# A float32 two-block transformer kernel: sixteen modulation chunks load into a buffer of their own

## The chip, the cores and the metric

The kernel runs on one core of a Trainium2 chip. The metric is device time in microseconds from the first to the last instruction of the core, with what the launch adds around it. The engines are TensorE (PE; its weight loads are PEld), VectorE (DVE), ScalarE (ACT), GpSimd (POOL) and SyncE (SP), whose queue issues nearly all of the weight transfers.

## The reference

Two blocks run over 256 positions of width 2048, all in float32: an attention block with an FFN, then an mLSTM block with a gated convolution. Both are modulated by a condition vector `c`. Of the first block, cut to what matters here:

```python
mod = silu(c) @ w_ada + b_ada
sh_a, sc_a, gt_a, sh_f, sc_f, gt_f = split(mod, 6)
h = rmsnorm(x, g_pre_attn) * (1 + sc_a) + sh_a
proj = h @ w_in                       # 2048 x 6144
mix = concat([dilated_attention(...), differential_attention(...)])
x = x + gt_a * rmsnorm(mix @ w_out, g_post_attn)
h = rmsnorm(x, g_pre_ffn) * (1 + sc_f) + sh_f
x = x + gt_f * rmsnorm((silu(h @ w_gate) * (h @ w_up)) @ w_down, g_post_ffn)
```

The product with `w_ada` is matrix times vector: its 96 chunks for this block (48 more belong to the second block) of 128 x 2048 floats are read once each.

## The kernel before

**Weights.** Every weight matrix comes as chunks of 1 MiB (128 partitions x 2048 floats) into one of four slots of the tile RAW. A chunk is two halves of 1024 columns. Each half is split in two parts so that float32 accuracy is kept: ACT copies it rounded into HI (`hi_half`, L668), DVE subtracts and writes the rest into LO (`split_half`, L1625), and TensorE does three products per half (`narrow`; HI with the high and the low part of the activations at L1200 and L1201, LO with the high part at L1209). HI and LO have four half-slots each, so ACT and DVE run at most four halves ahead of TensorE.

**Modulation.** A modulation chunk needs no TensorE: DVE multiplies it with the condition vector and sums over the row in one instruction, in place (`ada_chunk`, L1635), and adds 1 to the semaphore `ada_step`.

**Order.** `first_body()` writes out the order of the first section, "W" for a weight chunk and "A" for a modulation chunk. From chunk 16 on each W is followed by the A's that `ADA_BEHIND` gives it: one for chunks 18 to 61, two for 48, 50, 52 and 54. The class `Section` gives item j of that list the slot j mod 4; the load of an item waits until the item four places before it is used up (`slot_free`): by DVE's split for a W (`lo_ready`), by DVE's product for an A (`ada_step`). With W and A in turn, the four slots hold two of each. SP walks through the list in order: wait for the slot, issue the load, next item (`slot_wait`, `load` at L561). DVE walks through the same list: two splits for a W, and behind each half what else is due at that half (`beside_first(h)`); for an A its product.

**What else is due.** The first section has 64 weight chunks, halves 0 to 127. Halves 0 to 95 are the input projection, 96 to 127 the output projection. Beside them run the attention steps, placed by the half's number. Those that matter here: `rope` on DVE writes rotated queries and keys into QKY (two tiles of 1024 floats), TensorE turns them, ACT's `qk_evac` (L799) reads the turned ones out and adds 1 to `qt_ready` (16 in all, the last at half 88). `dilated_pv` (L1380) waits through `bank_7_free` until ACT has taken the head before (`dilated_out`, L850). `head_rstd` on DVE (L2000) precedes `head_norm` on ACT (L871), which precedes `mixa_turn` on TensorE (L1402), which precedes `mixa_hi` (L887) and on DVE `mixa_low` (L1899, halves 103 and 111). `out_gain` on DVE (L2015, halves 116 and 120) takes a group's outcome out of the two banks that TensorE's halves 116 and 120 start to fill again; TensorE waits for it (`wo_out`). At the end TensorE does the first 128 rows of halves 124 to 127 ahead of the second 128 rows.

**Memory.** The tile R is cut into regions by hand. QKY lies at 12288 to 14335. C_ROW_2, the condition of the second block, lies at 13312 and is loaded once the first section is over.

Of the kernel before, what the change touches and what calls it, by code (L numbers as in the profile page):

```python
# [52 lines left out]
RAWS = 4  # L53
HLS = 4
# [34 lines left out]
DIRECT_PAIRS = 6  # L89

ADA_BEHIND = sorted(list(range(18, 62)) + [48, 50, 52, 54])

UNITS_AT = 40

# [143 lines left out]
class Section:  # L238


    def __init__(self, plan, name, body, n_iter, groups=0):
        self.name, self.body, self.n_iter, self.groups = name, body, n_iter, groups
        self.n_chunks = len(body)
        self.n_halves = 2 * sum(kind == "W" for kind, *_ in body)
        self.n_ada = sum(kind == "A" for kind, *_ in body)
        assert self.n_chunks % RAWS == 0 and self.n_halves % HLS == 0
        self.chunk0, self.half0, self.ada0, self.group0 = plan.chunks, plan.halves, plan.ada, plan.groups
        self.items, half, ada = [], 0, 0
        slot_gain = [0] * RAWS
        for j, (kind, *what) in enumerate(body):  # L250
            slot = j % RAWS
            slot_gain[slot] += 16
            self.items.append(dict(kind=kind, what=what, slot=slot, j=j, half=half, ada=ada,
                                   landed=slot_gain[slot]))
            if kind == "W":
                half += 2
            else:
                ada += 1
        self.slot_gain = slot_gain
        self.landed0 = list(plan.landed)  # L260
        self.before = list(plan.last)
        n = n_iter
        plan.chunks += n * self.n_chunks
        plan.halves += n * self.n_halves
        plan.ada += n * self.n_ada
        plan.groups += n * groups
        for s in range(RAWS):
            plan.landed[s] += n * slot_gain[s]
        plan.last = [self.freed(self.items[j], n - 1) for j in range(self.n_chunks - RAWS, self.n_chunks)]

    def freed(self, it, i):

# [11 lines left out]
        return self.group0 + i * self.groups + off  # L284

    def landed(self, i, it):
        return self.landed0[it["slot"]] + i * self.slot_gain[it["slot"]] + it["landed"]

    def slot_free(self, i, it):
        j = it["j"] - RAWS  # L290
        if j >= 0:
            return self.freed(self.items[j], i)
        if isinstance(i, int) and i == 0:
            return self.before[it["j"]]
        return self.freed(self.items[self.n_chunks + j], i - 1)


class Plan:
    def __init__(self):
        self.chunks = self.halves = self.ada = self.groups = 0  # L300
        self.landed = [0] * RAWS
        self.last = [None] * RAWS


def first_body():

    body = [("A",)] * 4
    for n in range(8):
        ahead = [("A",)] * (2 if n < 7 else 0)
        if n == 0:  # L310
            body += [("W", 0)] + ahead + [("W", 1)] + ahead
            continue
        if n == 6:
            body += ahead + [("W", 2 * n), ("W", 2 * n + 1)] + ahead
            continue
        body += ahead + [("W", 2 * n)] + ahead + [("W", 2 * n + 1)]
    for c in range(16, 64):
        body.append(("W", c))
        body += [("A",)] * ADA_BEHIND.count(c)
    return body  # L320


# [39 lines left out]
def build(nc, x, c_rows, pos_cols, smalls, lambda_q1, lambda_k1, lambda_q2, lambda_k2,  # L362
# [4 lines left out]
    with ctx:  # L367
# [5 lines left out]
        def sem(name):  # L373
            return ctx.enter_context(nc.semaphore(name))

        PS = ctx.enter_context(nc.psum_tensor("PS", [P, 8, 512], F32))
        RAW = sb("RAW", [P, RAWS, 2048])
# [41 lines left out]
        def region(at, *shape):  # L419
            n = int(np.prod(shape))  # L420
            assert at + n <= RF, (at, shape)
            v = R[:, at:at + n]
            if len(shape) == 2:
                return v.rearrange("p (a b) -> p a b", a=shape[0])
            if len(shape) == 3:
                return v.rearrange("p (a b c) -> p a b c", a=shape[0], b=shape[1])
            return v
# [17 lines left out]
        MTB = region(8192, NH, S)  # L445
        GGA = region(10240, 2048)
        QKY = [region(12288 + 1024 * n, NT, 512) for n in range(2)]
        ROT = region(14336, 2, 512)
        JUNKW = region(14336, 2, 512)
        PX = region(15360, 4, 256)  # L450
# [51 lines left out]
            sum_m en_ready if_cols mq_ready ms_done w_x w_e pm_ready mpv_done mo_done  # L502
            zb_silu conv_in conv_t conv_y conv_ready o_sig h_gated mssq m_ms m_root m_rstd z_silu
            ha_ready hat_ready gates_sig merged merge_t mt_ready rows_2 sq_2 x_normf normf_in out_ready last_ready out_done""".split()
        landed = [sem(f"landed{i}") for i in range(RAWS)]
        bias_in = [sem(f"bias_in{i}") for i in range(4)]

        s = namedtuple("Semaphores", names)(*[sem(n) for n in names])
# [28 lines left out]
        def as_it_is(h):  # L537

            n, g = divmod(h, EARLY)
            return WHOLE[:, (n * len(DIRECT) + DIRECT.index(g)) % 4, :]  # L540

        def bank_of(g):
            return 2 * (g % 2)

# [13 lines left out]
        @block.sync  # L558
        def _(sp):
            def load(sec, it, chunk):  # L560
                sp.dma_start(RAW[:, it["slot"], :], chunk).then_inc(landed[it["slot"]], 16)  # L561

            def ada_dma(sec, it):
                load(sec, it, w_mod[sec.ada_chunk(0, it["ada"])])

            def slot_wait(sec, it):
                freed = sec.slot_free(0, it)
                if freed is not None:
                    sp.wait_ge({"W": s.lo_ready, "D": s.hi_ready, "A": s.ada_step}[freed[0]], freed[1])

            sp.dma_start(C_IN, c_rows[0:1, :]).then_inc(s.c_in, 16)
            sec = secs["first"]
            for it in sec.items:
                slot_wait(sec, it)
                if it["kind"] == "A":
                    ada_dma(sec, it)
                    if it["j"] == 0:
                        for u in range(NT):
                            sp.dma_start(X[:, u, :], x[0, u * P:(u + 1) * P, :]).then_inc((s.x_in, s.x_in_1)[u], 16)
                    continue  # L580
                load(sec, it, w_first[it["what"][0]])
            sec = secs["ffn"]
            for it in sec.items:
                slot_wait(sec, it)
                if it["kind"] == "A":
                    ada_dma(sec, it)
                    continue
                load(sec, it, w_ffn[it["half"] // 2])
            sec = secs["down"]
            for it in sec.items:  # L590
                slot_wait(sec, it)
                if it["kind"] == "A":
                    ada_dma(sec, it)
                    continue
                load(sec, it, w_down[it["what"][0]])
            sp.wait_ge(s.ada_step, ADA_OF_C)
            sec = secs["second"]
            for it in sec.items:
                g, k = it["what"]
                _, at = source_of(g)  # L600
                if k == 0 and g < PROJ_B:
                    if g >= 4:
                        sp.wait_ge(s.group_out, left(g - 4))
                    sp.dma_start(BIAS4[:, g % 4, :], b_in_2[0:1, at:at + 512].to_broadcast([P, 512]))\
                      .then_inc(bias_in[g % 4], 16)
                freed = sec.slot_free(0, it)
                sp.wait_ge(s.lo_ready if freed[0] == "W" else s.ada_step, freed[1])
                load(sec, it, w_second[it["half"] // 2])
            for n, (u, cols) in enumerate(((0, slice(0, 1024)), (0, slice(1024, 2048)), (1, slice(0, 512)), (1, slice(512, 1280)))):
                sp.wait_ge(s.out_ready, n + 1)  # L610
                sp.dma_start(out[0, u * P:(u + 1) * P, cols], X[:, u, cols]).then_inc(s.out_done, 16)
            sp.wait_ge(s.out_done, 80)
# [1000 lines left out]
        def _(dve):  # L1613
# [14 lines left out]
            def ada_chunk(sec, it):  # L1628

                a = sec.ada_chunk(0, it["ada"])  # L1630
                w = RAW[:, it["slot"], :]
                dve.wait_ge(landed[it["slot"]], sec.landed(0, it))
                if a == ADA_OF_C:
                    dve.wait_ge(s.cact_ready, 2)
                dve.tensor_tensor_reduce(w, w, C_ROW if a < ADA_OF_C else C_ROW_2, 1.0, 0.0, ALU.mult, ALU.add,  # L1635
                                         MOD[:, a:a + 1]).then_inc(s.ada_step, 1)
                for n, at in enumerate(GATE_AT):
                    if a == at + NK - 1:
                        gate(n)
                if a == MOD_AT[1] + 31:  # L1640
                    modulation(2)
# [188 lines left out]
            sec = secs["first"]  # L1830
# [270 lines left out]
            sec = secs["ffn"]  # L2101
# [18 lines left out]
            sec = secs["second"]  # L2120
# [253 lines left out]
            for h in range(HALVES_2 + EVAC):  # L2374
                g, n = divmod(h, 8)
# [135 lines left out]
```

## Time and profile before

| | us |
|---|---|
| median of 3 runs | 2382.34 (2380.48 to 2387.35) |
| the profiled execution | 2381.54 |
| its span, first to last instruction | 2379.7 |
| PE busy in the span | 2334.0 (98%) |
| DVE busy in the span | 1815.3 (76%) |
| ACT busy in the span | 1121.4 (47%) |
| transfers | 598.47 MB, 251 GB/s over the span |

A row of a page or a view has the line of the kernel behind an L, the engine, the operation and its tiles. An idle time in brackets is how long the engine stood still before the row, with what released it. A busy PE isn't PE at its peak: ends of matmuls are modelled.

### The profile page before, as it was taken

To read this page: it belongs to the slowest core of one execution; us is meant where nothing else is said; L and a number is where in the kernel's file an instruction comes from. 1 tells how busy PE (TensorE), PEld (TensorE's weight loads), DVE (VectorE), ACT (ScalarE), POOL (GpSimd) and SP (SyncE) were. 2 spreads that over 40 slices of the span, in tenths; PEclk is the share of its full clock that TensorE was granted. 3 is DMA by queue.
4 is the path that set the end of the run, shared out by engine and by line. 5 is a ranking of instruction groups with operands and counts; after the bars stand their busy time and mean duration, and the time that the engine had idled before them with its cause. 6 is when DMAs were issued, how large, how long until landed. Compare 5 with 4: busy or idle time off the path is not lost.

```text
span 2379.7 us, 26167 instructions
## 1 busy us (share of the span) xinstructions
PE 2334.0 (98%) x10274; PEld 1887.7 (79%) x10274; DVE 1815.3 (76%) x2441; ACT 1121.4 (47%) x1471; POOL 14.7 (1%) x31
## 2 busy tenths in 40 slices
PE   7999999999999999999999999999999999999998
PEld 3377787878888888888878888888888888888887
DVE  6698988878888888987665577998767795555775
ACT  5445566464444444444464434444345544444453
POOL 0000000000000000000000000000000000000000
PEclk8999999999999999999999999999999999999999
DMA  9988889877787777888746555555666657555553
GB/s 375 421 295 309 293 321 341 327 266 284 281 300 283 283 281 284 305 331 316 267 155 203 199 199 193 190 191 203 208 208 208 202 193 258 200 192 192 189 194 123
DMA packets 87757, 598.47 MB, mean 251 GB/s; under 512 B 10145, under 2 KB 10209, under 8 KB 16593
## 3 DMA queue, kind: packets, MB, share of 16 engines
q1 hardware_dynamic: 85538, 588.95, 68.8%
q0 software_dynamic: 1664, 7.19, 0.9%
q8 instruction: 81, 1.33, 0.2%
q10 hardware_dynamic: 432, 0.66, 0.1%
q14 instruction: 42, 0.34, 0.0%
HBM read 594.62 MB, written 2.13 MB: 251 GB/s over the span
## 4 chain that ended last, share of the span: by engine, by line
PE 89%; DVE 5%; DMA 4%; ACT 1%; issue 1%; DVEq 0%; ACTq 0%
PE PS L1184 20%; PE PS L1200 19%; PE PS L1201 19%; PE PS L1209 19%; PE PS L1189 10%; DVE RAW L1635 2%; DMA RAW<-in_w_first 2%; DMA RAW<-in_w_mod 2%; DVE LO L1625 1%; PE PS L1329 1%; PE PS L1548 0%; DVE X L1714 0%; ACT R L665 0%; ACT HI L668 0%; PE PS L1279 0%
## 5 line engine op out<-in xcount | busy, mean ns | idle before, releaser
L668 ACT ACTIVATE HI<-RAW 128x1024 fp32r<-128x1024 f32 x784 | 828.2, 1059 | 1096.0 <-PE PS L1209 669.2
L1625 DVE TENSOR_TENSOR LO<-RAW,HI 128x1024 fp32r<-128x1024 f32 x784 | 956.5, 1223 | 464.1 <-ACT HI L668 460.4
L1200 PE MATMUL PS<-HI,XH 128*128 128x512 f32 x2080 | 822.5, 395 | 4.9 <-DVE XL L1888 1.6
L1201 PE MATMUL PS<-HI,XL 128*128 128x512 f32 x2080 | 811.2, 390 | 0.0
L1209 PE MATMUL PS<-LO,XH 128*128 128x512 f32 x2080 | 559.1, 390 | 1.1 <-DVE LO L1625 1.1
L1200 PEld LDWEIGHTS PS<-HI,XH 128*128 128x128 f32 x2080 | 390.8, 188 | 90.1 <-DVE XL L1888 4.0
L1209 PEld LDWEIGHTS PS<-LO,XH 128*128 128x128 f32 x2080 | 391.0, 188 | 83.5 <-DVE LO L1625 1.6
L1201 PEld LDWEIGHTS PS<-HI,XL 128*128 128x128 f32 x2080 | 391.1, 188 | 79.0
L1184 PE MATMUL PS<-HI,XH 128*128 128x512 f32 x1056 | 325.9, 390 | 1.6 <-DVE XL L1735 1.1
L1184 PE MATMUL PS<-HI,XL 128*128 128x512 f32 x1056 | 325.2, 389 | 0.0
L1189 PE MATMUL PS<-LO,XH 128*128 128x512 f32 x1056 | 283.9, 389 | 0.0
L1635 DVE CUSTOM_DVE_ANT_0 RAW<-RAW,BIAS 128x2048 f32<-128x2048 f32 x96 | 218.9, 2287 | 32.7 <-DMA RAW<-in_w_mod 24.3
L1665 DVE STREAM_TRANSPOSE R<-R 32x256 f32<-32x256 f32 (+1 forms) x608 | 230.8, 380 | 12.7
L1184 PEld LDWEIGHTS PS<-HI,XH 128*128 128x128 f32 x1056 | 197.7, 188 | 42.6 <-DVE XL L1735 1.3
L1184 PEld LDWEIGHTS PS<-HI,XL 128*128 128x128 f32 x1056 | 198.3, 188 | 41.2
L1189 PEld LDWEIGHTS PS<-LO,XH 128*128 128x128 f32 x1056 | 198.2, 188 | 41.3 <-DVE LO L1625 0.2
L1635 DVE CUSTOM_DVE_ANT_0 RAW<-RAW,R 128x2048 f32<-128x2048 f32 x48 | 109.9, 2289 | 0.5
L1224 PE MATMUL PS<-R 128*128 128x512 f32 x192 | 87.1, 609 | 7.9 <-ACT XH L787 5.0
L1224 PEld LDWEIGHTS PS<-R 128*128 128x128 f32 x192 | 36.5, 194 | 58.0 <-issue 52.2
L665 ACT ACTIVATE R<-RAW 128x1024 f32<-128x1024 f32 x24 | 24.1, 1048 | 45.9 <-DMA RAW<-in_w_first 45.8
L2307 DVE TENSOR_TENSOR R<-PS,BIAS 128x1024 f32<-128x1024 f32 x24 | 29.2, 1216 | 0.0
L737 ACT ACTIVATE R<-PS,MOD,SCALE 128x256 f32<-128x256 f32 (+1 forms) x38 | 18.0, 525 | 14.4 <-PE PS L1279 14.4
(258 smaller groups left out, 876.2 us busy)
## 6 DMA issues: line engine op xcount, KB each, us to landing
RAW<-in_w_second SPq DMA_DIRECT2D x208, 1024.0 KB, 4.8
RAW<-in_w_mod SPq DMA_DIRECT2D x144, 1024.0 KB, 5.5
RAW<-in_w_ffn SPq DMA_DIRECT2D x88, 1024.0 KB, 4.9
RAW<-in_w_first SPq DMA_DIRECT2D x64, 1024.0 KB, 6.2
RAW<-in_w_down SPq DMA_DIRECT2D x44, 1024.0 KB, 5.1
BIAS<-in_b_in SPq DMA_DIRECT2D x40, 256.0 KB, 5.1
R<-mod_rows POOLq DMA_DIRECT2D x3, 1024.0 KB, 7.4
X<-in_x SPq DMA_DIRECT2D x2, 1024.0 KB, 8.8
```

The lines of the kernel that those rows point to most:

```text
L665: act.activation(as_it_is(h), whole, ACT.Copy).then_inc(s.hi_ready, 1)
L668: act.activation(HI[:, (it["half"] + hf) % HLS, :], whole, ACT.Copy).then_inc(s.hi_ready, 1)
L1184: pe.matmul(PS[:, bank_of(u, cc), :], x, HI[:, slot, cc * 512:(cc + 1) * 512], start=first and x is xh, stop=False)
L1189: m = pe.matmul(PS[:, bank_of(u, cc), :], XH[:, slot_k, u * P:(u + 1) * P], LO[:, slot, cc * 512:(cc + 1) * 512], start=False, stop=last)
L1200: pe.matmul(PS[:, bank + u, :], XH[:, 2 * n + kk, rows], hi, start=start and kk == 0, stop=False)
L1201: pe.matmul(PS[:, bank + u, :], XL[:, 2 * n + kk, rows], hi, start=False, stop=False)
L1209: m = pe.matmul(PS[:, bank + u, :], XH[:, 2 * n + kk, u * P:(u + 1) * P], lo, start=False, stop=stop and kk == 1)
L1224: m = pe.matmul(PS[:, bank + u, :], XT[:, 2 * n + kk, u * P:(u + 1) * P], as_it_is(h)[:, kk * 512:(kk + 1) * 512], start=start and kk == 0 ...
L1625: dve.tensor_tensor(LO[:, slot, :], RAW[:, it["slot"], hf * 1024:(hf + 1) * 1024], HI[:, slot, :].bitcast(F32), ALU.subtract).then_inc(s.l ...
L1635: dve.tensor_tensor_reduce(w, w, C_ROW if a < ADA_OF_C else C_ROW_2, 1.0, 0.0, ALU.mult, ALU.add, MOD[:, a:a + 1]).then_inc(s.ada_step, 1)
L1665: m = dve.transpose(columns(b, a), rows(a, b))
L2307: dve.tensor_tensor(dst, y, bias, ALU.add).then_inc(s.group_out, 1)
```

## The change

Sixteen modulation chunks, the first one behind each of the weight chunks 44 to 59, are loaded into a buffer of their own, OWN, at 12288 in R (where QKY lies). The class `Plan` keeps a turn over the four slots for all other items of all sections; the fifth slot, with a semaphore of its own, is OWN. Each item carries the count at which it has landed and what must be used up before its load. SP skips an OWN item in the list and issues its load behind the load of weight chunk c+2; before the first it waits for `qt_ready` 16, before each of the others for the product of the OWN chunk before it. The order of DVE, ACT and TensorE is unchanged. The number of other items in the first section is 128, so later sections keep their slots.

```diff
--- before.py
+++ after.py
@@ -90,6 +90,8 @@
 
 ADA_BEHIND = sorted(list(range(18, 62)) + [48, 50, 52, 54])
 
+OWN_SLOT = range(44, 60)
+
 UNITS_AT = 40
 
 
@@ -243,30 +245,28 @@
         self.n_chunks = len(body)
         self.n_halves = 2 * sum(kind == "W" for kind, *_ in body)
         self.n_ada = sum(kind == "A" for kind, *_ in body)
-        assert self.n_chunks % RAWS == 0 and self.n_halves % HLS == 0
+        assert self.n_halves % HLS == 0
         self.chunk0, self.half0, self.ada0, self.group0 = plan.chunks, plan.halves, plan.ada, plan.groups
         self.items, half, ada = [], 0, 0
-        slot_gain = [0] * RAWS
         for j, (kind, *what) in enumerate(body):
-            slot = j % RAWS
-            slot_gain[slot] += 16
-            self.items.append(dict(kind=kind, what=what, slot=slot, j=j, half=half, ada=ada,
-                                   landed=slot_gain[slot]))
+            if kind == "A" and what:
+                slot = RAWS
+            else:
+                slot = plan.turn % RAWS
+                plan.turn += 1
+            plan.landed[slot] += 16
+            it = dict(kind=kind, what=what, slot=slot, j=j, half=half, ada=ada, landed=plan.landed[slot], free=plan.last[slot])
+            self.items.append(it)
+            plan.last[slot] = self.freed(it, 0)
             if kind == "W":
                 half += 2
             else:
                 ada += 1
-        self.slot_gain = slot_gain
-        self.landed0 = list(plan.landed)
-        self.before = list(plan.last)
         n = n_iter
         plan.chunks += n * self.n_chunks
         plan.halves += n * self.n_halves
         plan.ada += n * self.n_ada
         plan.groups += n * groups
-        for s in range(RAWS):
-            plan.landed[s] += n * slot_gain[s]
-        plan.last = [self.freed(self.items[j], n - 1) for j in range(self.n_chunks - RAWS, self.n_chunks)]
 
     def freed(self, it, i):
 
@@ -284,22 +284,18 @@
         return self.group0 + i * self.groups + off
 
     def landed(self, i, it):
-        return self.landed0[it["slot"]] + i * self.slot_gain[it["slot"]] + it["landed"]
+        return it["landed"]
 
     def slot_free(self, i, it):
-        j = it["j"] - RAWS
-        if j >= 0:
-            return self.freed(self.items[j], i)
-        if isinstance(i, int) and i == 0:
-            return self.before[it["j"]]
-        return self.freed(self.items[self.n_chunks + j], i - 1)
+        return it["free"]
 
 
 class Plan:
     def __init__(self):
         self.chunks = self.halves = self.ada = self.groups = 0
-        self.landed = [0] * RAWS
-        self.last = [None] * RAWS
+        self.landed = [0] * (RAWS + 1)
+        self.last = [None] * (RAWS + 1)
+        self.turn = 0
 
 
 def first_body():
@@ -316,7 +312,9 @@
         body += ahead + [("W", 2 * n)] + ahead + [("W", 2 * n + 1)]
     for c in range(16, 64):
         body.append(("W", c))
-        body += [("A",)] * ADA_BEHIND.count(c)
+        if c in OWN_SLOT:
+            body.append(("A", c))
+        body += [("A",)] * (ADA_BEHIND.count(c) - (c in OWN_SLOT))
     return body
 
 
@@ -445,6 +443,7 @@
         MTB = region(8192, NH, S)
         GGA = region(10240, 2048)
         QKY = [region(12288 + 1024 * n, NT, 512) for n in range(2)]
+        OWN = region(12288, 2048)
         ROT = region(14336, 2, 512)
         JUNKW = region(14336, 2, 512)
         PX = region(15360, 4, 256)
@@ -502,7 +501,7 @@
             sum_m en_ready if_cols mq_ready ms_done w_x w_e pm_ready mpv_done mo_done
             zb_silu conv_in conv_t conv_y conv_ready o_sig h_gated mssq m_ms m_root m_rstd z_silu
             ha_ready hat_ready gates_sig merged merge_t mt_ready rows_2 sq_2 x_normf normf_in out_ready last_ready out_done""".split()
-        landed = [sem(f"landed{i}") for i in range(RAWS)]
+        landed = [sem(f"landed{i}") for i in range(RAWS + 1)]
         bias_in = [sem(f"bias_in{i}") for i in range(4)]
 
         s = namedtuple("Semaphores", names)(*[sem(n) for n in names])
@@ -539,6 +538,9 @@
             n, g = divmod(h, EARLY)
             return WHOLE[:, (n * len(DIRECT) + DIRECT.index(g)) % 4, :]
 
+        def raw_of(it):
+            return OWN if it["slot"] == RAWS else RAW[:, it["slot"], :]
+
         def bank_of(g):
             return 2 * (g % 2)
 
@@ -558,7 +560,7 @@
         @block.sync
         def _(sp):
             def load(sec, it, chunk):
-                sp.dma_start(RAW[:, it["slot"], :], chunk).then_inc(landed[it["slot"]], 16)
+                sp.dma_start(raw_of(it), chunk).then_inc(landed[it["slot"]], 16)
 
             def ada_dma(sec, it):
                 load(sec, it, w_mod[sec.ada_chunk(0, it["ada"])])
@@ -570,7 +572,10 @@
 
             sp.dma_start(C_IN, c_rows[0:1, :]).then_inc(s.c_in, 16)
             sec = secs["first"]
+            own = {it["what"][0]: it for it in sec.items if it["slot"] == RAWS}
             for it in sec.items:
+                if it["slot"] == RAWS:
+                    continue
                 slot_wait(sec, it)
                 if it["kind"] == "A":
                     ada_dma(sec, it)
@@ -579,6 +584,12 @@
                             sp.dma_start(X[:, u, :], x[0, u * P:(u + 1) * P, :]).then_inc((s.x_in, s.x_in_1)[u], 16)
                     continue
                 load(sec, it, w_first[it["what"][0]])
+                c = it["what"][0] - 2
+                if c in own:
+                    if c == OWN_SLOT[0]:
+                        sp.wait_ge(s.qt_ready, 16)
+                    slot_wait(sec, own[c])
+                    ada_dma(sec, own[c])
             sec = secs["ffn"]
             for it in sec.items:
                 slot_wait(sec, it)
@@ -1628,7 +1639,7 @@
             def ada_chunk(sec, it):
 
                 a = sec.ada_chunk(0, it["ada"])
-                w = RAW[:, it["slot"], :]
+                w = raw_of(it)
                 dve.wait_ge(landed[it["slot"]], sec.landed(0, it))
                 if a == ADA_OF_C:
                     dve.wait_ge(s.cact_ready, 2)
```

## Rows read from the trace of the kernel before

**Rows 1.** The page, part 1: busy time of each engine.
```profile
PE 2334.0 (98%) x10274; PEld 1887.7 (79%) x10274; DVE 1815.3 (76%) x2441; ACT 1121.4 (47%) x1471; POOL 14.7 (1%) x31
```

**Rows 2.** Busy time by stretch: stretch, length, engines, granted clock, DMA share, GB/s.
```profile
345.50:390.50 45.00, 42.82 (x231) 36.35 (x229) 37.87 (x58) 33.35 (x77) 0.00 (x0) 1.00 0.87 324
390.50:449.70 59.20, 56.69 (x258) 46.48 (x256) 52.06 (x54) 29.33 (x58) 0.00 (x0) 1.00 0.97 368
449.70:466.20 16.50, 16.50 (x74) 13.69 (x73) 14.64 (x15) 7.26 (x10) 0.00 (x0) 1.00 0.97 359
```

**Rows 3.** Waits of PE from 330 to 470 us: total, times, longest.
```profile
PE PS L1380 <- ACT R L850: 2.2, 1, 2.2
PE PS L1402 <- ACT R L871: 1.4, 1, 1.4
PE PS L1200 <- DVE XL L1899: 1.1, 1, 1.1
```

**Rows 4.** Timeline, all engines, 380 to 410 us: start, length, instruction, idle before it.
```profile
380.02 2.29 DVE L1635 CUSTOM_DVE_ANT_0 RAW<-RAW,BIAS 128x2048 f32<-128x2048 f32 x1
...
382.35 0.33 SPq L561 DMA_DIRECT2D RAW<-in_w_first  x1
...
384.93 0.33 SPq L561 DMA_DIRECT2D RAW<-in_w_mod  x1
...
387.24 1.06 ACT L668 ACTIVATE HI<-RAW 128x1024 fp32r<-128x1024 f32 x1 [0.98 <-DMA RAW<-in_w_first]
...
409.45 1.06 ACT L668 ACTIVATE HI<-RAW 128x1024 fp32r<-128x1024 f32 x1 [4.18 <-DMA RAW<-in_w_first]
```

**Rows 5.** Loads: modulation from 500 to 900, from 400 to 430; RAW from 370 to 420.
```profile
RAW<-in_w_mod SPq DMA_DIRECT2D x34, 1024.0 KB, 4.9
...
RAW<-in_w_mod SPq DMA_DIRECT2D x6, 1024.0 KB, 7.7
...
DMA to landing us min/median/max: 4.8/6.5/8.6
```

**Rows 6.** Timeline of DVE: first modulation products behind chunks 44, 48, 50, 52, 54, 55, 59.
```profile
342.05 2.29 DVE L1635 CUSTOM_DVE_ANT_0 RAW<-RAW,BIAS 128x2048 f32<-128x2048 f32 x1
...
371.65 2.28 DVE L1635 CUSTOM_DVE_ANT_0 RAW<-RAW,BIAS 128x2048 f32<-128x2048 f32 x1
...
384.83 2.28 DVE L1635 CUSTOM_DVE_ANT_0 RAW<-RAW,BIAS 128x2048 f32<-128x2048 f32 x1
...
399.41 2.28 DVE L1635 CUSTOM_DVE_ANT_0 RAW<-RAW,BIAS 128x2048 f32<-128x2048 f32 x1
...
413.14 2.28 DVE L1635 CUSTOM_DVE_ANT_0 RAW<-RAW,BIAS 128x2048 f32<-128x2048 f32 x1
...
422.21 2.28 DVE L1635 CUSTOM_DVE_ANT_0 RAW<-RAW,BIAS 128x2048 f32<-128x2048 f32 x1
...
443.21 2.29 DVE L1635 CUSTOM_DVE_ANT_0 RAW<-RAW,BIAS 128x2048 f32<-128x2048 f32 x1
```

**Rows 7.** Timeline of SP and ACT from 337 to 340 us.
```profile
337.12 0.33 SPq L561 DMA_DIRECT2D RAW<-in_w_first  x1
...
338.23 0.58 ACT L799 ACTIVATE R<-PS 128x512 f32<-128x512 f32 x1
...
339.33 0.33 SPq L561 DMA_DIRECT2D RAW<-in_w_mod  x1
```

**Rows 8.** Timeline of DVE and PE from 446 to 450 us.
```profile
446.97 1.23 DVE L1625 TENSOR_TENSOR LO<-RAW,HI 128x1024 fp32r<-128x1024 f32 x1 [1.47 <-ACT HI L668]
448.12 1.22 DVE L2015 TENSOR_TENSOR R<-PS,R 128x1024 f32<-128x1024 f32 x1
...
449.68 0.39 PE L1200 MATMUL PS<-HI,XH 128*128 128x512 f32 x1
```

**Rows 9.** A gap of PE earlier in the section, and the busy time behind it.
```profile
168.40 0.63 PE L1318 MATMUL PS<-SMALLS,R 128*128 128x128 f32 x4 [3.07 <-ACT R L799]
...
170.00:175.00 5.00, 5.00 (x19) 3.98 (x18) 5.00 (x5) 2.13 (x4) 0.00 (x0) 0.71 0.99 395
```

## Prediction

> **What bounds the kernel now.** I read first how busy TensorE is, then where it stands idle near the change, then who made it wait. Over the execution PE is 98% busy [rows 1]. The change touches the first section's last 40 of 128 halves (a chunk of weights is two halves), so I cut the trace there, at TensorE's starts of halves 88, 100 and 120. From 345.5 to 390.5 us twelve halves take 45.0 us, from 390.5 to 449.7 twenty take 59.2 us, all of it at a granted clock of 1.00 [rows 2]. Per chunk that is 7.5 us in the first stretch (attention lies between the products) and 5.92 us in the second. TensorE idles 2.18 us and 2.51 us in them, and not at all in the eight halves behind. The waits name the same places: 2.2, 1.4 and 1.1 us, 4.7 us together [rows 3]. So TensorE sets the pace, with DVE three or four halves ahead of it, and all that could be won in this region is 4.7 us, 0.2%. What can be lost is larger, because DVE is nearly as full (37.9 of 45.0 and 52.1 of 59.2 us [rows 2]) and runs strictly in order: splits of the weights, modulation chunks, attention.
>
> **What the change removes and adds.** The 16 modulation products themselves (L1635, 2.29 us each with the read of the sum) stay on DVE in the same places of its order. Bytes stay the same. Removed: sixteen of the turns in the four slots, so a weight chunk can be loaded up to four weight chunks ahead instead of two. Added: one single buffer for the sixteen, and on SP, in order, a wait for the previous modulation product before each of their loads. SP issues each such load behind weight chunk c+2, but in effect the wait sets its time: the buffer is free only when the product of c-1 is done.
>
> That makes a closed cycle of steps that can't overlap: product, SP's issue, the load, product. The load is the unknown. Its nearest rows: the product that started at 380.02 us released SP, which issued at 382.35 (2.33 us later), and ACT started on that chunk at 387.24 [rows 4]. That is 4.89 us from the issue to its reader's start, although the queue got another load 2.58 us behind it, which is how the new loads will lie. The median of the modulation loads in the FFN section, with one or two loads in flight, is 4.9 us as well; in the crowded stretch from 400 to 430 us it is 7.7 us, because three or four loads queue up there [rows 5]. I take the 4.89, and keep 4.5 and 7.7 for the range. One cycle is then 2.33 + 4.89 = **7.22 us**. Beside TensorE's 7.5 us per chunk it costs nothing; beside 5.92 us it costs 1.3 us per chunk until DVE's lead is gone, and then all of it is TensorE's.
>
> The Trainium skill, "Trainium Kernel Development and Optimization", Best Practices, says to double-buffer so that transfers and compute overlap; a buffer of one, refilled behind its own reader, is the opposite, and the rows above say what that costs here. The Trainium skill, "DMA: Bandwidth & Descriptors", Anatomy of one DMA, fits 2.0 us plus the bytes at 436 GB/s; for 1 MiB that is an estimate of 4.4 us, by which the sum below would be about 8 us. The trace's 4.89 us is used.
>
> **The walk through the sixteen.** Starts of before are the L1635 rows [rows 4, 6]. DVE's work between them keeps its durations: a split takes 1.14 us from start to start, a product 2.2.
> Chunk 44: SP issues W46 at 337.12 and can issue again 2.2 us later, at 339.33, as in before; the last rotated keys have left the buffer at 338.8 (L799, 338.23 + 0.58) [rows 7]. DVE starts at 344.2 against 342.05, +2.2. Four cycles lead to 373.1 for chunk 48, against 371.65, +1.4: the pace there is 7.5 us and the lead hides it. Chunk 48 has a second product in an ordinary slot, and from 48 to 49 DVE has 8.4 us of work of its own, more than a cycle: chunk 49 at 381.5, again +1.5.
> Chunk 50: released at 383.8, started at 388.7, where DVE was ready at 386.3; **+3.9**. On TensorE's side the wait at L1380 may grow: the attention norms on ACT start behind DVE's L2000, some 1.5 us late now, less the 0.98 us that ACT waited for a weight chunk [rows 4] and that the longer look-ahead removes. Chunk 51 by DVE's own work (two products, two splits, two clamps, L1899): 398.0, again +3.8. Chunk 52 by the cycle: 405.2 against 399.41, **+5.8**. Chunk 53, by either, 412.6, +5.7. Chunk 54 by the cycle: 419.8 against 413.14, **+6.7**. Chunk 55 by DVE's own work (two products, two splits, L1899): 427.8 against 422.21, +5.6. TensorE's half 110 waits for that L1899 and is now as late as it.
> Chunks 56 to 59 by the cycle, four times 7.22: 456.7 against 443.21, **+13.5**.
> Then comes the gate that turns this into time. TensorE's half 120, started at 449.68, needs the outcome of DVE's L2015, which ended at 449.3 (448.12 + 1.22) [rows 8]: 0.4 us of slack. Between chunk 59's product and it, DVE idled 1.47 us for ACT [rows 8], and that is eaten first. So half 120 starts 13.5 - 1.47 - 0.4 = **11.6 us** later, at 461.3. The eight halves behind it are back to back in before [rows 2] and stay so, since DVE's own backlog behind the gate, two products and seven splits among it, keeps its length. Everything further is bound by the same chains as before and shifts as a whole; the FFN section has no idle in which to win it back.
>
> What costs nothing, and why: the weight loads come earlier than needed (each is issued at the latest one cycle after its slot, two chunks ahead of use); the wait for the last rotation falls at 338.8, in SP's ordinary pause; the rotation buffer has no other reader after that. ACT's waits for weight chunks vanish, but ACT isn't late except at the L1380 place already counted. The cycle decides at some eight places (50, 52, 53, 54, 56 to 59), so each tenth of a microsecond in the landing moves the sum by 0.8 us.
>
> **The sum** against the profiled execution: 2381.5 + 11.6 = 2393.1. That execution was 0.8 us under the median of the three runs, so by the median 2393.9.
>
> **Rivals.**
> *The longer look-ahead wins (not slower).* If each modulation load landed before DVE reached it, the 2.2 us and parts of the 1.4 and 1.1 us would go: up to 4.7 us less, 2378. For it: ahead of both longer waits ACT had waited for a weight chunk, 0.98 us at 387.24 and 4.18 us at 409.45 [rows 4]. Its point: the cycle would have to be no longer than 5.92 us, so a landing within 3.6 us; no load of weights or modulation from 370 to 420 us landed in under 4.8 us [rows 5]. Chance 0.05.
> *Mostly hidden (slower by less than 7 us).* Landings near 4.2 us, or more of DVE's lead left than I count: 11.6 less 0.8 us per tenth, so 2384 to 2389. Against it stands the same 4.8 us. Chance 0.11.
> *More than forecast.* The new loads meet the weight loads and take 6.5 us, the median from 370 to 420 us [rows 5]: 1.6 us times eight, 2407. Or TensorE's clock falls in the new gaps: after a gap of 3.07 us before 168.40 us the granted clock was 0.71 in the next five [rows 9], while around the gap of 2.2 us in the region it stayed at 1.00 [rows 2, 3]. My gaps are 1 to 3 us; at 0.71 five microseconds lose 1.5, mostly inside time in which TensorE waits anyway. Chance 0.15.
> *The change doesn't do what it says.* The slots don't hold weights alone: four modulation chunks (the second ones of 48, 50, 52, 54) and the last two stay in them, and W45 and W47 still wait for one. It changes no number above.
>
> **How the numbers follow.** Forecast 0.69, with its own range 2391 to 2399 (landing 4.5 to 5.5 us). About 0.3% (7 us) is what a measurement of this kernel tells from no change. Faster by more than that would need more than all the idle there is: 0.02. Within it: most of the first two rivals, 0.14. Slower: 0.84. The range 2387 to 2406 leaves out the first rival, most of the second and the far end of the third.
>
> **What would show it.** In the changed kernel the waits "DVE RAW L1635 from the modulation load" (0.3 us in the region before) should become some 20 us over ten times or more, up to 2.6 us each; the L1635 starts of chunks 56 to 59 should be 7.2 us apart; TensorE should idle 12 to 14 us from half 100 to half 120, not 2.5; ACT's waits for weights of the first section should be near nothing there; half 120 should start at 461 us. I am wrong if the L1635 starts keep a spacing of 5 to 6 us in the last chunks, or if half 120 is late and the end is not.

## The result and the profile after

The changed kernel takes 2411.0 us (median of 4 runs, 2409.8 to 2413.3) against 2383.2 for the kernel before in the same rounds: ratio 1.0121, 95% interval 1.0109 to 1.0133. The ratio makes 28.8 us (these two medians differ by 27.8), where I had forecast 11.6 and a range that ended at 2406. The profiled execution took 2410.6 us with a span of 2408.8, 29.1 more than the span before. Of all executions below one was disturbed, the profiled one of the kernel that keeps TensorE busy: it took 7650 us, the other three 2409 to 2411, and it is left out.

In the changed kernel the lines behind L540 have moved: the product on DVE is L1646 (was L1635), the split L1636 (L1625), the low part of the mixed heads L1910 (L1899), the gain L2026 (L2015), the attention norms L882 (L871), the transposes on TensorE L1391 and L1413 (L1380 and L1402).

The page, part 1, answers to [rows 1]: all engines do the same work in a longer span.

```profile
PE 2341.8 (97%) x10274; PEld 1892.7 (79%) x10274; DVE 1815.6 (75%) x2441; ACT 1122.1 (47%) x1471; POOL 14.7 (1%) x31
```

TensorE's waits of the changed kernel from 330 to 500 us (total, times, longest), which answer to [rows 3]:

```profile
PE PS L1413 <- ACT R L882: 8.7, 1, 8.7
PE PS L1391 <- ACT R L861: 7.0, 2, 6.1
PE PS L1211 <- DVE R L2026: 6.6, 2, 4.5
PE PS L1371 <- DVE SMALL L1946: 1.0, 1, 1.0
PE PS L1211 <- DVE XL L1910: 0.7, 1, 0.7
PE PS L1220 <- DVE LO L1636: 0.5, 1, 0.5
```

They sum to 24.5 us where there were 4.7. Behind nearly all of them stands one wait of DVE, in the same stretch (0.3 us and one time before):

```profile
DVE R L1646 <- DMA R<-in_w_mod: 39.3, 15, 4.9
```

So 15 of the 16 products find their chunk not landed. The longest of TensorE's waits, for instance, comes from there (DVE, ACT and TensorE):

```profile
425.42 2.29 DVE L1646 CUSTOM_DVE_ANT_0 R<-R,BIAS 128x2048 f32<-128x2048 f32 x1 [4.91 <-DMA R<-in_w_mod]
...
429.20 2.44 ACT L882 ACTIVATE R<-R,SMALL 128x128 f32<-128x128 f32 x8 [7.57 <-DVE SMALL L2011]
...
431.70 1.97 PE L1413 MATMUL PS<-SMALLS,R 128*128 128x128 f32 x8 [8.69 <-ACT R L882]
```

DVE waited 4.91 us for the load of this product, `head_rstd` (L2011) follows it on DVE, the norm on ACT waits for that and TensorE for the norm. The next view shows why some of these waits are longer than others. It is the timeline from 368 to 400 us, of SP's issues and DVE's products (start, length, instruction, idle before it and who ended it):

```profile
370.38 0.33 SPq L563 DMA_DIRECT2D R<-in_w_mod  x1
...
375.11 2.29 DVE L1646 CUSTOM_DVE_ANT_0 R<-R,BIAS 128x2048 f32<-128x2048 f32 x1 [0.81 <-DMA R<-in_w_mod]
...
377.33 2.29 DVE L1646 CUSTOM_DVE_ANT_0 RAW<-RAW,BIAS 128x2048 f32<-128x2048 f32 x1
...
379.65 0.33 SPq L563 DMA_DIRECT2D RAW<-in_w_first  x1
...
380.03 0.43 SPq L563 DMA_DIRECT2D R<-in_w_mod  x1
...
387.18 2.29 DVE L1646 CUSTOM_DVE_ANT_0 R<-R,BIAS 128x2048 f32<-128x2048 f32 x1 [3.71 <-DMA R<-in_w_mod]
...
389.51 0.33 SPq L563 DMA_DIRECT2D R<-in_w_mod  x1
...
394.37 2.29 DVE L1646 CUSTOM_DVE_ANT_0 R<-R,BIAS 128x2048 f32<-128x2048 f32 x1 [2.30 <-DMA R<-in_w_mod]
```

Read it from the top. The load for chunk 48's product out of OWN is issued at 370.38 and used at 375.11, 4.73 us later. Its product ends at 377.4, and OWN is free. But SP issues the next load into OWN only at 380.03, 2.6 us later. It stood behind weight chunk 51 (379.65), which waits for a slot that the next product, the one on RAW at 377.33, sets free at 379.6. And now the load lies directly behind that weight chunk: it is used 7.15 us after its issue, not 4.73. The load at 389.51 has nothing close in front of it (the nearest was issued 6.4 us earlier) and takes 4.86 us again. The same pair of delays comes back with weight chunk 53 (398.90, and OWN's load at 399.28 is used at 406.08) and with chunk 55 (417.91, 418.28, used at 425.42).

At the end of the section (timeline of DVE and PE):

```profile
470.48 2.29 DVE L1646 CUSTOM_DVE_ANT_0 R<-R,BIAS 128x2048 f32<-128x2048 f32 x1 [3.94 <-DMA R<-in_w_mod]
...
473.84 1.22 DVE L2026 TENSOR_TENSOR R<-PS,R 128x1024 f32<-128x1024 f32 x1
...
475.11 0.80 PE L1211 MATMUL PS<-HI,XH 128*128 128x512 f32 x1 [4.53 <-DVE R L2026]
```

Chunk 59's product starts at 470.48, 27.3 us after that of [rows 6], and TensorE's half 120 at 475.11, 25.4 us after that of [rows 8]. The stretch from there until TensorE has done the first 128 rows of halves 124 to 127 took 16.50 us in before [rows 2]; now it is

```profile
475.11:493.88 18.77, 18.77 (x73) 15.34 (x74) 14.95 (x15) 5.36 (x8) 0.00 (x0) 0.88 0.85 309
```

with no idle and a granted clock of 0.88: 2.3 us more. That leaves 29.1 - 25.4 - 2.3 = 1.4 us further on, which I haven't placed.

### The profile page after: what moved, and what is told of

Same layout as the page of the kernel before. It is cut to its first block, busy times and chain, and to the rows that moved or that the text cites. A ratio compares the mean times of both kernels' runs of the same rounds, so it can differ in the third digit from the quotient of the medians.

```text
span 2408.8 us, 26167 instructions
## 1 busy us (share of the span) xinstructions
PE 2341.8 (97%) x10274; PEld 1892.7 (79%) x10274; DVE 1815.6 (75%) x2441; ACT 1122.1 (47%) x1471; POOL 14.7 (1%) x31
## 4 chain that ended last, share of the span: by engine, by line
PE 85%; DMA 6%; DVE 6%; ACT 2%; issue 1%; SPq 0%; DVEq 0%; ACTq 0%
PE PS L1195 20%; PE PS L1211 18%; PE PS L1212 18%; PE PS L1220 18%; PE PS L1200 10%; DMA R<-in_w_mod 3%; DVE RAW L1646 2%; DMA RAW<-in_w_mod 2%; DMA RAW<-in_w_first 1%; DVE R L1646 1%; PE PS L1340 1%; DVE LO L1636 0%; PE PS L1559 0%; DVE X L1725 0%; ACT R L676 0%
## 5 line engine op out<-in xcount | busy, mean ns | idle before, releaser
L1636 DVE TENSOR_TENSOR LO<-RAW,HI 128x1024 fp32r<-128x1024 f32 x784 | 956.8, 1224 | 453.2 <-ACT HI L679 449.6
L1646 DVE CUSTOM_DVE_ANT_0 RAW<-RAW,BIAS 128x2048 f32<-128x2048 f32 x80 | 182.7, 2288 | 32.5 <-DMA RAW<-in_w_mod 24.2
L1646 DVE CUSTOM_DVE_ANT_0 RAW<-RAW,R 128x2048 f32<-128x2048 f32 x48 | 109.9, 2289 | 0.5
L1646 DVE CUSTOM_DVE_ANT_0 R<-R,BIAS 128x2048 f32<-128x2048 f32 x16 | 36.7, 2292 | 39.3 <-DMA R<-in_w_mod 39.3
```

The source lines that it names most:

```text
L1636: dve.tensor_tensor(LO[:, slot, :], RAW[:, it["slot"], hf * 1024:(hf + 1) * 1024], HI[:, slot, :].bitcast(F32), ALU.subtract).then_inc(s.l ...
```

## The experiments

Times are medians, ratios are to the kernel before, run beside them on the same chip; c is the number of the weight chunk that a modulation chunk stands behind. All diffs are against the changed kernel.

| kernel | us | ratio, 95% interval |
|---|---|---|
| changed kernel, again | 2411.8 | 1.0113 to 1.0144 |
| all sixteen loads ahead of weight chunk c+2 | 2399.9 | 1.0061 to 1.0091 |
| only three of them ahead | 2401.1 | 1.0065 to 1.0099 |
| second product of a pair in OWN | 2400.2 | 1.0067 to 1.0097 |
| loads issued by GpSimd | 2410.8 | 1.0106 to 1.0134 |
| a quarter of each load | 2388.0 | 1.0014 to 1.0036 |
| every second chunk | 2425.3 | 1.0163 to 1.0197 |
| every second chunk, in its own place | 2378.2 | 0.9974 to 0.9993 |
| two buffers | 2393.8 | 1.0035 to 1.0065 |
| two buffers, loads ahead | 2383.0 | 0.9993 to 1.0010 |
| only the four second chunks in OWN | 2379.1 | 0.9979 to 0.9996 |
| TensorE kept busy in the last gaps (three runs) | 2410.6 | 1.0106 to 1.0140 |

**The order on SP.** OWN's loads go ahead of weight chunk c+2:

```diff
             for it in sec.items:
                 if it["slot"] == RAWS:
                     continue
+                if it["kind"] == "W" and it["what"][0] - 2 in own:
+                    ...                      # wait for OWN, issue its load
                 slot_wait(sec, it)
...
                 load(sec, it, w_first[it["what"][0]])
-                c = it["what"][0] - 2
-                if c in own:
-                    ...
```

> Only the order on SP differs from the changed kernel: each load into OWN is issued ahead of weight chunk c+2, not behind it. Theory A (queue order adds to the cycle of the single buffer): in the changed kernel three of these loads (behind chunks 49, 51, 53) waited on SP until the weight chunk ahead of them had its slot, some 2.3 us, and then landed 2.3 us later because that chunk's bytes go first (7.15, 6.8, 7.1 us against 4.86). Both go: 3 x 4.6 = 14 us less, about 2397, with landings of 4.9 us throughout and cycles of 7.2 us. Rival B (the cycle alone with the attention chain on ACT and TensorE's lower clock behind the gaps makes the time, and the order is harmless): within 3 us of the changed kernel's 2411. Rival C (the weight loads now come too late, ACT waits): slower than 2411.

Measured: 2399.9, 11 us less than the changed kernel, so theory A; rivals B (no difference) and C (slower) fall. Not all of the 14 us came, and landings were not 4.9 us throughout. The timeline shows one that wasn't:

```profile
353.23 0.33 SPq L563 DMA_DIRECT2D R<-in_w_mod  x1
...
353.60 0.43 SPq L563 DMA_DIRECT2D RAW<-in_w_first  x1
...
354.07 0.44 SPq L563 DMA_DIRECT2D RAW<-in_w_mod  x1
...
358.12 2.29 DVE L1646 CUSTOM_DVE_ANT_0 R<-R,BIAS 128x2048 f32<-128x2048 f32 x1 [2.03 <-DMA R<-in_w_mod]
...
360.45 0.33 SPq L563 DMA_DIRECT2D R<-in_w_mod  x1
...
360.82 0.43 SPq L563 DMA_DIRECT2D RAW<-in_w_first  x1
...
366.81 2.29 DVE L1646 CUSTOM_DVE_ANT_0 R<-R,BIAS 128x2048 f32<-128x2048 f32 x1 [3.09 <-DMA R<-in_w_mod]
```

The first load, ahead of two others, is used after 4.89 us. The next one is issued 7.2 us later and is used after 6.36: of the three loads before it the last, issued at 354.07, takes 9.0 us to land and is still on its way. The slowest is chunk 51's load, issued at 392.98: it takes 7.6 us to land, behind one issued at 387.57 that takes 8.9. In these traces a follower on SP's queue costs a load nothing; a predecessor that hasn't landed does.

Then only the three loads that were held up:

```diff
-                if c in own:
+                if c in own and c not in (49, 51, 53):
...
+                if it["kind"] == "W" and it["what"][0] in (51, 53, 55):
+                    ...
```

> The changed kernel with only the three held-up loads (behind chunks 49, 51 and 53) issued ahead of weight chunk c+2; the other thirteen keep their place. Theory E: these three places carry the whole cost of the order, so the time is that of the run with all sixteen ahead (2400) or a little less, 2396 to 2401. If the order costs something at every place, 2405 to 2409.

2401.1, at the upper end of what I expected: within the noise these three places carry the whole cost of the order. The third run reaches them by another way. It turns the two modulation chunks of a pair round, so that the slot is freed by the earlier product:

```diff
         body.append(("W", c))
-        if c in OWN_SLOT:
-            body.append(("A", c))
         body += [("A",)] * (ADA_BEHIND.count(c) - (c in OWN_SLOT))
+        if c in OWN_SLOT:
+            body.append(("A", c))
```

> The changed kernel with the two modulation chunks behind 48, 50, 52 and 54 in the other order: the first goes through a slot, the second through OWN. The slot that weight chunks 51, 53 and 55 wait for is now freed by the earlier product, so SP issues them 2.2 us before OWN is free, and the load into OWN follows when its own product is done. Theory E: neither held up nor directly behind the weight chunk's bytes, 2398 to 2404. If only the cycle of product and landing matters: as the changed kernel, 2411.

2400.2. SP's list is as in the changed kernel, only the weight chunk is no longer held until OWN is long free. Three kernels agree within 1.3 us on 11 us for the order.

**The cycle.** What is left, some 18 us over the kernel before, should be the single buffer's cycle with its landings. First the landing time, shortened: the kernel leaves out three quarters of each of the sixteen loads, so their sixteen modulation values are wrong, while all other work stays.

```diff
+                chunk = w_mod[sec.ada_chunk(0, it["ada"])]
+                if it["slot"] == RAWS:
+                    sp.dma_start(OWN[:, 0:512], chunk[:, 0:512]).then_inc(landed[RAWS], 16)
+                    return
```

> The changed kernel with only the first 512 of 2048 columns of each of the sixteen chunks loaded; the products run over the whole buffer, so the sixteen modulation values are left wrong and the rest of the work is the same. Theory A: landing of a load that nothing precedes falls from 4.9 to about 3 us, so the cycle is 5.3 us, under TensorE's 5.92; the three loads that are held behind a weight chunk keep most of their delay (a cycle near 10 us there). Time 2385 to 2392. Rival D (landing time alone is the cause, the order adds nothing): equal to the kernel before or up to 4.7 us under it, 2378 to 2383. Rival B (attention chain and clock): above 2400.

2388.0, as theory A had it: shorter landings take 23 us off, and 5.6 us over the kernel before stay, where rival D had none. That these 5.6 us are the order's is likely but not shown by itself: in the three held-up places the quarter loads still took 5.2 to 5.4 us to land, elsewhere mostly 2.8 to 3.5. This run also moves 12 MiB less, so it shows landing time and traffic together. Then the same loads on another queue:

```diff
             gate_rows(0, GGA)
+            pool.wait_ge(s.qt_ready, 16)
+            for it in secs["first"].items:
+                if it["slot"] == RAWS:
+                    ...                      # pool.wait_ge(s.ada_step, ...)
+                    pool.dma_start(OWN, w_mod[...]).then_inc(landed[RAWS], 16)
```

> The changed kernel with its sixteen loads issued from GpSimd, which does nothing else then, so they never stand behind a weight chunk's slot on SP; the single buffer and its wait for the product before stay. This leaves the closed cycle alone. Theory E plus cycle: near the run with the loads ahead (2400), 2393 to 2401, with cycles of 7 to 8 us. If the cycle weren't a cause of its own: under 2388. If it were the whole: 2411.

2410.8, a miss: I expected 2393 to 2401. Two of its loads, with what was issued near them and the products that use them:

```profile
386.44 0.33 SPq L563 DMA_DIRECT2D RAW<-in_w_first  x1
...
389.40 0.53 POOL L643 DMA_DIRECT2D R<-in_w_mod  x1 [7.86 <-DVE MOD L1646]
...
391.72 0.33 SPq L563 DMA_DIRECT2D RAW<-in_w_mod  x1
...
396.80 2.29 DVE L1646 CUSTOM_DVE_ANT_0 R<-R,BIAS 128x2048 f32<-128x2048 f32 x1 [5.11 <-DMA R<-in_w_mod]
...
453.39 0.53 POOL L643 DMA_DIRECT2D R<-in_w_mod  x1 [9.79 <-DVE MOD L1646]
...
455.40 0.33 SPq L563 DMA_DIRECT2D RAW<-in_w_mod  x1
...
458.47 2.29 DVE L1646 CUSTOM_DVE_ANT_0 R<-R,BIAS 128x2048 f32<-128x2048 f32 x1 [3.10 <-DMA R<-in_w_mod]
```

Nothing but the product of the chunk before holds up the issue (the one at 386.80 released that at 389.40, 2.6 us later), but two things are dearer than on SP's queue. The shortest cycle is longer: the last four products start at 450.80, 458.47, 466.25 and 473.93, 7.7 to 7.8 us apart instead of 7.1 to 7.2, because the issue comes 2.6 us after the product's start and the load takes at least 5.1 us to its use. And some of SP's loads are still on their way when one of OWN's is issued: the load at 389.40 takes 7.4 us with a weight chunk issued 3.0 us ahead of it on the other queue, and those at 338.48, 424.63 and 443.08 take 8.8, 7.9 and 7.7 us to land, each with two such loads on their way. A load that SP issues behind it doesn't do that by itself: the one at 453.39 has one 2.0 us behind it and is used after 5.08 us. How much each of the two costs in time isn't shown, so this run doesn't isolate the cycle.

**One refill per two chunks.** Two ways: use OWN for every second chunk only, or have two buffers.

```diff
-OWN_SLOT = range(44, 60)
+OWN_SLOT = range(44, 60, 2)
```

> The changed kernel with OWN used by every second of the sixteen chunks (8 loads; the other 8 go through the four slots as in the kernel before). One refill now has two chunks of TensorE's time, 11.8 us, against a cycle of 7.2 to 9.9 us. Theory A and theory of the single buffer: the loss is gone, 2380 to 2386, waits of DVE for OWN near zero. If the slots without modulation chunks were themselves a cost (weights loaded too early or late), half of the loss would stay, about 2396.

2425.3, the worst of all, where I had expected 2380 to 2386, with the buffer free for a whole chunk before each refill. DVE waited up to 8.9 us for a load. This overthrew the idea that the single buffer alone sets the time. With more modulation chunks back in the four slots, the item whose slot weight chunk c+2 needs is late: for 48 to 54 it is weight chunk c itself, for the others the product of c-1. SP, which has to issue that chunk first, comes to OWN's load for c when the halves of c are split, and its product is the next thing DVE does. Chunk 50's:

```profile
398.30 0.33 SPq L563 DMA_DIRECT2D RAW<-in_w_first  x1
...
398.67 0.43 SPq L563 DMA_DIRECT2D R<-in_w_mod  x1
...
406.64 2.29 DVE L1646 CUSTOM_DVE_ANT_0 R<-R,BIAS 128x2048 f32<-128x2048 f32 x1 [8.37 <-DMA R<-in_w_mod]
```

The test of that: the same buffer for every second chunk, with its load in its own place in SP's list, behind weight chunk c and ahead of c+1 (from chunk 46 on, so that SP isn't held up by the rotations):

```diff
-OWN_SLOT = range(44, 60)
+OWN_SLOT = range(46, 60, 2)
...
                 if it["slot"] == RAWS:
+                    if it["what"][0] == OWN_SLOT[0]:
+                        sp.wait_ge(s.qt_ready, 16)
+                    slot_wait(sec, it)
+                    ada_dma(sec, it)
                     continue
```

> Every second chunk (46 to 58, seven of them) in the one buffer OWN, and its load issued in its own place of SP's list, behind weight chunk c and ahead of c+1; compared with the run of every second chunk, where it stood behind c+2 and the time was 2425. Theory E: the buffer has been free for more than a chunk when SP gets there, so the load is as early as in the kernel before; 2380 to 2387. Theory F, or a cost of the single buffer itself: above 2400.

2378.2, 47 us less than its twin, which began two chunks earlier, and below the 2380 to 2387 that I had expected. All of TensorE's waits from 330 to 470 us are now

```profile
PE PS L1388 <- ACT R L858: 1.1, 1, 1.1
PE PS L1410 <- ACT R L879: 0.3, 1, 0.3
```

where [rows 3] had 4.7 us, and no product waits for a load. Against the kernel before it is 0.17% faster, with an interval that ends below 1.

The two buffers, the second of them at 6144 in R, free behind the last score; chunks 48 to 59 alternate:

```diff
-OWN_SLOT = range(44, 60)
+OWN_SLOT = range(48, 60)
...
-                slot = RAWS
+                slot = RAWS + what[0] % 2
...
-        OWN = region(12288, 2048)
+        OWN = [region(12288, 2048), region(6144, 2048)]
```

> Chunks 48 to 59 alternate between OWN and a second buffer at 6144 in the same tile (keys of the last heads, free after the last score), so each refill waits for the product two chunks back; 44 to 47 go through the slots. Theory A: no cycle and no exposed landing, DVE waits for neither buffer; 2378 to 2384. If the longer look-ahead of the weights is worth anything, this shows it: down to 4.7 us under the kernel before. Rival B: the gaps of TensorE stay in part, above 2390.

2393.8, 10 us over the end of what I expected: DVE still waits 19.6 us, at nine products, because the loads still stand behind c+2. With the loads ahead of it:

> The two-buffer kernel with its loads issued ahead of weight chunk c+2 instead of behind it. Theory E (what counts is when SP comes to issue the load: behind weight chunk c+2 it stands behind that chunk's slot, which four times is freed by a modulation product just done, and behind its bytes): every load is issued when the product two chunks back is done, at least 5 us before DVE needs it; DVE's waits for these buffers fall from 19.6 us to under 5, time 2379 to 2384. Theory F (the slots holding mostly weights are themselves the loss): stays at 2390 or more.

2383.0 (ratio 0.9993 to 1.0010), and DVE's waits for these loads are 4.8 us. Theory E holds, theory F (slots that hold mostly weights cost something) falls. The step from one buffer to two, both with the loads ahead, is 17 us: that is what the cycle costs, all but isolated, for chunks 44 to 47 differ too.

**The look-ahead itself.** Only the four second chunks go to OWN, each ahead of weight chunk c+1, and the slots keep their turn:

```diff
-OWN_SLOT = range(44, 60)
+OWN_SLOT = (48, 50, 52, 54)
```

> Only four modulation chunks use OWN, the second ones behind 48, 50, 52 and 54, each issued ahead of weight chunk c+1; all else goes through the slots, which now keep their turn of weight and modulation. Theory E: one refill per two chunks is hidden, and the weight loads at 396 and 409 us of the kernel before, for which ACT waited 4.1 and 4.2 us, come earlier; TensorE's 4.7 us of idle there shrink to 1 to 3: 2379 to 2382, at best 0.15% under the kernel before. If the idle there is set by DVE's own work: no difference.

2379.1 (0.9979 to 0.9996), TensorE's waits are 1.6 us instead of 4.7. So the 3 us that can be had here come with the four pairs alone, which had pushed the weight loads back: ACT's waits for weight chunks from 385 to 415 us (0.98, 4.05 and 4.18 us) are down to one of 0.24. A look-ahead over four weight chunks isn't needed for it.

**The clock.** 32 small transposes ahead of the wait at half 120 and 8 ahead of half 116:

```diff
                     if h in (116, 120):
+                        keep_busy(7, 8 if h == 116 else 32)
                         pe.wait_ge(s.wo_out, 1 if h == 116 else 2)
```

> The changed kernel with 32 small transposes on TensorE (3.8 us, by the 1.91 us that 16 take) ahead of its wait at half 120, where it stood idle for 4.53 us and where the next half ran at a granted clock of 0.53, and 8 ahead of half 116. Theory G (the lower clock behind that gap made 2.3 us of the 29): 2.0 to 2.5 us less than the changed kernel, 2408.6. If the lower clock is hidden behind DVE: no difference; if the transposes delay half 120: up to 1 us more.

> The changed kernel itself once more, on the same chip as the three beside it, as their measure: 2411.

2410.6 against 2411.8 for the changed kernel beside it, three runs of the one and four of the other, spread over 2 and 4 us. The 1.2 us between them is told neither from zero nor from the 2.0 to 2.5 us that theory G had. The kernel with the transposes left no trace that can be set beside the others, so nothing says whether the clock stayed up in it. The changed kernel's second trace shows the low clock again: there half 120's products start at 477.99 and take 4.4 us, in the first trace 5.1, before 2.7. That a lower clock took 1.7 to 2.4 us behind the last gap stands as a reading of two traces, and its part in the time is open.

## Why the prediction was wrong

The direction and the mechanism were right: a single buffer, refilled behind its own reader, makes a cycle; DVE's lead hides it up to chunk 48; the gate at half 120 turns the delay into time. These steps came out as follows.

- **The cycle of 7.22 us.** Right where nothing that is still on its way was issued in front: from chunk 55 to 58 the products start at 440.58, 447.67, 454.78 and 461.96, 7.1 to 7.2 us apart, and a load is used 4.7 to 4.9 us after its issue. As a rule for all sixteen it was mis-sized: chunk 44's load took 6.42 us, chunk 47's 6.25, chunk 59's 6.19, each behind others. In the kernel with all loads ahead, where the cycle and its landings are left, the time is 17.5 us over the kernel before (2399.9 against 2382.4), 6 more than my 11.6. Its product for chunk 59 starts at 462.55; I had 456.7, again 6 us. That the two agree so well is partly luck: its profiled execution is 20.0 us longer than the one before, 2.5 of them behind half 120.
- **The step that failed:** "SP issues each such load behind weight chunk c+2, but in effect the wait sets its time". For chunks 49, 51 and 53 it doesn't. I had listed as a rival that four modulation chunks remain in the slots and wrote "It changes no number above". It changed the number by 11 us: three of them, behind 48, 50 and 52, are the chunks whose products free the slots of weight chunks 51, 53 and 55, and SP stands there with OWN's load behind it. My own row of the list, "each is issued at the latest one cycle after its slot", looked at the weight loads and not at what is queued behind them. Forecast and measured starts of the products show it: chunk 48 373.1 and 375.11, chunk 49 381.5 and 387.18, chunk 50 388.7 and 394.37, chunk 51 398.0 and 406.08, chunk 52 405.2 and 413.36, chunk 53 412.6 and 425.42, chunk 54 419.8 and 432.69, chunk 59 456.7 and 470.48. The error is 2.0 us at chunk 48 (the landings of 44 and 47), jumps at 49, 51 and 53 by 3.7, 2.4 and 4.7 us, and grows by 1 us more up to 59. Three kernels without that hold-up lie 11 us lower.
- **"a load 2.58 us behind it costs nothing"** was right on SP's queue. I had taken it to say that the loads don't disturb each other; a load in front that hasn't landed does, by 2.3 us when it is issued 0.4 us ahead.
- **The gate.** 27.3 us at chunk 59, less the 1.47 and 0.4 us [rows 8], makes 25.4, and half 120 started 25.4 us late. This part of the working was exact.
- **"shifts as a whole"** was out by 3.7 us, of which by the trace 2.3 lie in the lower clock behind the last gap (the run with TensorE kept busy could neither confirm nor refute it). I had called such gaps at most 3 us; they were 6.1, 8.7 and 4.5.
- **The bounds.** The rival "more than forecast" had a landing of 6.5 us as its cause and ended at 2407; I had no case in which the issue itself is held up, so the range ended too early. In sum, for the profiled executions: 11.6 as forecast, 13.8 more by the product of chunk 59 (470.48 against 456.7) and 3.7 behind half 120 make the 29.1. Of the 13.8 the three held-up places make 10.7 and the slow landings of 44, 47 and 59 most of the rest. Taking the hold-up away moved that product by 7.9 us only, since other loads then landed late (7.6 and 6.9 us for chunks 51 and 59), though the medians differ by 11; single executions lie some us apart (those of the changed kernel from 2409.6 to 2413.8).
- **The rival "the longer look-ahead wins"** had a true part: 3 us of TensorE's 4.7 can be had, with OWN for four chunks or for seven.

The formula that the prediction cited (4.4 us for 1 MiB, an estimate from the Trainium skill, "DMA: Bandwidth & Descriptors", Anatomy of one DMA) lies 0.3 to 0.5 us under the shortest times here from issue to use, 4.73 to 4.9 us. That page of the Trainium skill fits it to DMAs that GpSimd issues; those took at least 5.1 us to their use here, 0.7 more.

## What to carry to other kernels

When a transfer gets a buffer of its own, write down for each one when the queue that issues it comes to it: the buffer being free is only one of its waits, and every wait of what stands ahead in that queue is another. A refill belongs in the list where its buffer is free and nothing that waits stands in front; moving it there was worth 11 us with one buffer, 11 us with two and 47 us with every second chunk (a run that also began two chunks later). One buffer refilled behind its reader costs reader plus landing per item (7.2 us here), so use it only for items further apart than that.

## What the hardware showed that I had not expected

A 1 MiB load on SP's queue with none on its way in front is used 4.7 to 5.2 us after its issue whatever is issued behind it, even 0.4 us behind, but 7.15 us after it with 1 MiB issued 0.4 us ahead. Issued from GpSimd, the same load takes 0.3 us more at best: 5.1 to 5.3 us to its use with nothing on its way in front, also with a load that SP issued 2.0 us later. It took 7.4 to 8.8 us to land in four places where loads that SP had issued 2 to 6 us before it were still on their way, but 5.5 us in two where one issued 3.8 or 4.9 us before it was. So a follower on the other queue doesn't by itself make a load late here; how much of the delay comes from what lies in front, and how much from both together, no run separates.
